# Attention with split-precision products: projection tiles of the next heads two to a pair of steps

## What is computed

```
z = rms_norm(x) @ w_in                      # q, k, v of all heads, gates, ...
q, k = rms_norm(q) * gq, rms_norm(k) * gk   # per head
c = cumsum(log_sigmoid(f + b))              # decay
s = q @ k.T * scale + (c[q] - c[k]), causal
attn = softmax(s) @ v
gates = g_a, g_b = two blocks of 1024 columns of z (sigmoid later)
```

## Time and profile before

| | |
|---|---|
| median of three runs | 1944.1 us (1943.78 to 1945.9) |
| profiled execution | 1945.08 us, span in the trace 1943.4 us |
| TensorE products busy | 1894.3 us, 97% of the span, 11188 instructions |
| VectorE, ScalarE, GpSimd busy | 962.5, 677.1, 520.9 us (50, 35, 27%) |
| TensorE on the chain that ended last | 83% |
| granted clock of TensorE | 0.999 |
| mean traffic | 92 GB/s |

### The profile page before, as it was taken

The page is one execution under the profiler, slowest core; times in us unless marked ns, Lnnn a source line. Parts: engine busy times, 40 slices in busy tenths (PEclk is TensorE's granted clock), DMA queues, the critical chain, the costliest instruction groups (busy, mean ns, idle before and its releaser), DMA issues.

```text
span 1943.4 us, 30986 instructions
## 1 busy us (share of the span) xinstructions
PE 1894.3 (97%) x11188; PEld 1746.3 (90%) x11188; DVE 962.5 (50%) x2296; ACT 677.1 (35%) x1487; POOL 520.9 (27%) x525
## 2 busy tenths in 40 slices
PE   5999999999999999999999999999999999999998
PEld 4999999999888889998889999999998888999986
DVE  5546665653265335545444565665433643455531
ACT  5344444444233223113224444444433332221210
POOL 3623343332031113212134233333311211131110
PEclk9999999999999999999999999999999999999999
DMA  5231313123225323625314113131322342227141
GB/s 157 57 109 49 94 52 98 53 71 88 80 59 141 91 62 87 202 80 172 105 50 116 52 48 100 45 107 49 104 62 62 92 137 77 77 86 232 39 173 54
DMA packets 217803, 178.39 MB, mean 92 GB/s; under 512 B 50260, under 2 KB 191076, under 8 KB 217652
## 3 DMA queue, kind: packets, MB, share of 16 engines
q1 hardware_dynamic: 217652, 176.41, 31.2%
HBM read 131.65 MB, written 44.71 MB: 91 GB/s over the span
## 4 chain that ended last, share of the span: by engine, by line
PE 83%; DVE 5%; issue 4%; DMA 3%; ACT 3%; POOL 1%; SPq 1%; POOLq 0%; DVEq 0%; ACTq 0%
PE bank L76 22%; PE bank L78 21%; PE bank L77 21%; PE bank L1345 3%; PE bank L1359 2%; PE bank L1305 2%; PE bank L1358 2%; PE bank L1328 2%; PE bank L2128 2%; PE bank L1330 2%; PE bank L2151 1%; DVE sg_sT L1583 1%; DMA at_stage<-in_w_in 1%; DVE at_prob L1225 1%; PE bank L2116 1%
## 5 line engine op out<-in xcount | busy, mean ns | idle before, releaser
L76 PE MATMUL bank<-keep_hhi,at_fhi 128*128 128x384 f32 (+1 forms) x768 | 257.1, 335 | 4.3 <-ACT at_th L993 4.0
L78 PE MATMUL bank<-keep_hhi,at_flo 128*128 128x384 f32 (+1 forms) x768 | 251.3, 327 | 0.0
L77 PE MATMUL bank<-keep_hlo,at_fhi 128*128 128x384 f32 (+1 forms) x768 | 251.3, 327 | 0.0
L76 PE MATMUL bank<-aw_whi,keep_hhi 128*128 128x384 f32 (+3 forms) x576 | 198.5, 345 | 3.2 <-ACT at_th L993 1.3
L76 PE MATMUL bank<-keep_hhi,bw_whi 128*128 128x384 f32 (+1 forms) x576 | 195.1, 339 | 2.6 <-DVE br_th L2016 2.6
L77 PE MATMUL bank<-aw_wlo,keep_hhi 128*128 128x384 f32 (+3 forms) x576 | 195.5, 339 | 0.0
L78 PE MATMUL bank<-aw_whi,keep_hlo 128*128 128x384 f32 (+3 forms) x576 | 195.2, 339 | 0.0
L77 PE MATMUL bank<-keep_hlo,bw_whi 128*128 128x384 f32 (+1 forms) x576 | 188.4, 327 | 0.0
L78 PE MATMUL bank<-keep_hhi,bw_wlo 128*128 128x384 f32 (+1 forms) x576 | 188.3, 327 | 0.0
L1039 ACT ACTIVATE at_prob<-at_prob,at_nmx 128x128 f32<-128x128 f32 (+7 forms) x128 | 99.5, 778 | 238.5 <-DVE at_nmx L1232 238.4
L76 PEld LDWEIGHTS bank<-keep_hhi,at_fhi 128*128 128x128 f32 x768 | 144.4, 188 | 7.7 <-ACT at_th L993 6.4
(11 more groups left out here) (252 smaller groups left out, 4283.9 us busy)
## 6 DMA issues: line engine op xcount, KB each, us to landing
at_stage<-in_w_in SPq DMA_DIRECT2D x160, 128.0 KB, 2.3
mg_gate<-gates SPq DMA_DIRECT2D x32, 544.0 KB, 6.2
gates<-at_th SPq DMA_DIRECT2D x64, 192.0 KB, 2.3
br_stage<-in_w_in SPq DMA_DIRECT2D x40, 256.0 KB, 3.2
at_stage<-in_w_in SPq DMA_DIRECT2D x48, 192.0 KB, 2.7
at_decay<-ncum SPq DMA_DIRECT2D x16, 512.0 KB, 3.7
br_k<-in_cache_k SPq DMA_DIRECT2D x32, 256.0 KB, 3.1
br_v<-in_cache_v SPq DMA_DIRECT2D x32, 256.0 KB, 2.9
```

The lines of the kernel that those rows point to most:

```text
L76: nc.tensor.matmul(out, sh, mh, start=start and i == 0, stop=False)
L77: nc.tensor.matmul(out, sh, ml, start=False, stop=False)
L78: last = nc.tensor.matmul(out, sl, mh, start=False, stop=stop and i == n - 1)
```

## The change

For head pairs 1 to 3 the nine projection tiles are due at the steps 3, 5, 7 ... 19 of 24 before, and at 11, 11, 13, 13, 15, 15, 17, 17, 19 after. The X of a tile is due with the next tile, as before, so two X are now due in some pairs. The first of them stays in front of the following T, the second goes behind the two T. W and Y keep their steps (their rule counts from the last tile's step, 19 in both). P moves by itself, by the straight-line rule.

```diff
@@ -679,7 +679,7 @@
     for p in range(1, PAIRS):
-        at = [3, 5, 7, 9, 11, 13, 15, 17, 19]
+        at = [11, 11, 13, 13, 15, 15, 17, 17, 19]
         for t, n in zip(range(NT - len(at), NT), at):
@@ -699,11 +699,13 @@
     for n in range(0, len(steps) + LAG, 2):
         due = after.pop(n, []) + after.pop(n + 1, [])
-        plan += turned
+        plan += turned[:1]
+        second = turned[1:]
         turned = [s for s in due if s[0] == "X"]
         scores = [s for s in due if s[0] == "S"]
         projections = [s for s in due if s[0] == "Z"]
         plan += [("T",) + s for s in steps[n:n + 2]]
+        plan += second
         fill.read(0)
```

## The result

| | before | after |
|---|---|---|
| median of four executions | 1944.0 us (1943.8 to 1945.9) | 2064.2 us (2061.0 to 2070.0) |
| ratio of the runs | 1 | 1.062 (95% interval 1.061 to 1.063) |
| span of the profiled execution | 1943.4 us | 2063.3 us |
| TensorE busy, mean granted clock | 1894.3 us, 0.999 | 1932.8 us, 0.979 |

What follows compares the result with a forecast made beforehand. TensorE, nearly never idle, was taken as the bound, each new wait adding in full. 48.8 + 16.4 + 6.2 + 9.0 = 80.4 us on a 1943.4 us span gave, after small corrections, 2024.5 us; range 1994 to 2042.

Steps and rivals of the forecast that it cites:

- What bounds the kernel: Attention, layers 0 and 1: TensorE nearly never idle, 8.4 us at most to win; each new wait adds in full.
- One sign of being wrong altogether: TensorE's busy time was forecast unchanged; a change in the busy sum would make the prediction wrong altogether.
- Part 1, the second X: X2, X4, X6 wait for the previous X's low part: 8.14 us per 24 steps, six times, 48.8 us.
- taking would have given 40.2: Second-X cost using the 3.13 us chain where GpSimd has nothing queued behind X, instead of 3.61 us: 40.2 us.
- Part 2, thin pairs: Pairs at 20 to 24 lack P, so T waits for late ScalarE and VectorE: 16.4 + 6.2 us; bounds 0, 32.
- the 0.3 us on the half output: In the thin pairs, 0.3 us more for a later wait on the head's half output, beside the 3.8 us wait.
- no P at 22: Claim that the filler, ahead after five dense pairs, puts no P at 22, where two or three stood before.
- Part 3, pairs filled with P: At n = 2, 6, 32 two G splits share a pair, delaying the tanh: 9.0 us both layers; bounds 0, 20.
- the rival that I gave 0.03: TensorE's clock at half rate for the P piece behind each of 14 waits over 3 us: 28 us, 2052; chance 0.03.
- only the second X costs: Rival: ScalarE's backlog is absorbed since TensorE arrives later everywhere; 40 to 49 us, 1984 to 1993; chance 0.12.
- the second X is hidden behind two T: Not-slower rival: low part comes within 1.23 us of the first X; near 1940 us; chance 0.04.
- The third, ScalarE blocked by loads in the filled pairs: Rival: loads block ScalarE's queue in all filled pairs, or late engines drag on; 101 us, about 2045; chance 0.10.

Runs made afterwards that it cites:

- The run with the low part first: Changed kernel, VectorE taking the low parts of an X ahead of evacuating the projection tile directly before it; TensorE's order kept: 2022.8 us (1.041).
- G later: Changed kernel with each split of gate weights listed behind the next pair's T and tanh reads instead of directly behind its P: 2044.3 us (1.051).
- W later: Changed kernel with splits of projection and value weights (W, Y) behind the next pair's T copies instead of ahead of them: 2050.4 us (1.053).
- the filled waits: Changed kernel with 12 or 10 additional 128x512 products on TensorE directly ahead of each second X, results overwritten: 2047.1 us (1.052).
- the artificial ones: Kernel before with ten TensorE waits added per layer, each for 12 or 22 GpSimd writes: 1962.2 us (1.009) and 2002.3 us (1.029).

## Why the prediction was right or wrong

**What bounds the kernel: right.** Each new wait of TensorE was added in full; the account above closes within 0.5 us. One sign of being wrong altogether did come: I had said that the busy time is unchanged, and it grew by 38.5 us. The products are the same; the clock and the hidden parts of the waits made them longer.

**Part 1, the second X: right, to the term.** 8.14 us for 24 steps, 48.8 us; measured 2.82 + 2.28 + 2.27 and three times 0.25, 48.7 us for all six. The rows to read it from were those of the rows phase's end, where the same order of tiles already stood; taking would have given 40.2. In all 18 of these waits `ms` takes 0.63 us and ends with `zg`. That fits the Trainium skill's rule on the port pair that VectorE and GpSimd share (SBUF — State Buffer, "Who interferes with whom"), by which the one that comes second is blocked until the other's instruction is over. No run takes `zg` out of the way, so the 8.6 us that this makes of the 48.8 rest on the durations alone. The run with the low part first shows the main cause: the order on VectorE.

**Part 2, thin pairs: mechanism right, size too high.** 22.6 us forecast, 15.1 measured. In layer 0 the three waits were 3.24, 1.10 and 2.48 us idle, 0.25 us more each with the hidden part, against 3.8, 3.8 and 3.1; the 0.3 us on the half output didn't come. The second is short because the list has one P at n = 46 after all: I carried "no P at 22" from the first 24 steps to the second, where the filler has caught up. The first, at 240.83, is as told:

```profile
238.02 1.35 ACT L970 ACTIVATE aw_whi<-at_stage 128x392 fp32r<-128x392 f32 x3
...
238.99 1.27 DVE L1151 TENSOR_TENSOR aw_wlo<-at_stage,aw_whi 128x392 fp32r<-128x392 f32 x1
...
239.84 0.55 ACT L1051 ACTIVATE at_pthi<-bank 128x256 fp32r<-128x256 f32 x2
...
240.83 0.92 PE L1347 MATMUL bank<-keep_ident,at_prob 128*128 128x128 f32 x4 [3.24 <-DVE at_ptlo L1243]
```

**Part 3, pairs filled with P: mechanism right, far too small.** 9.0 us forecast, 24.2 measured, above my own upper bound of 20. The one wait that I worked out is there, 1 us longer in layer 0 (4.18 us and the hidden 0.25 against 3.4; 2.94 us idle in layer 1). The release came where I had it (141.1 forecast), though I took 136.58, where the second half of the load starts to be issued in the earlier trace rows, for its end. TensorE was there 0.6 us sooner than I had it:

```profile
134.40 0.62 ACT L977 ACTIVATE at_fhi<-at_stage 128x512 fp32r<-128x512 f32 x1
...
139.26 0.63 ACT L977 ACTIVATE at_fhi<-at_stage 128x512 fp32r<-128x512 f32 x1 [3.08 <-DMA at_stage<-in_w_in]
139.79 1.06 ACT L1051 ACTIVATE at_pthi<-bank 128x512 fp32r<-128x512 f32 x2
...
140.75 0.82 ACT L995 ACTIVATE at_th<-bank 128x320 f32<-128x320 f32 x2
...
141.24 0.45 PE L76 MATMUL bank<-keep_hhi,at_fhi 128*128 128x384 f32 x1 [4.18 <-ACT at_th L995]
```

What failed is the choice of places. I asked where two G fall into one pair, and took 0.7 us for n = 6 and 32, which show 0.26 us and nothing in layer 0. The other waits lie at n = 26, 28, 48 and 52: 1.2, 2.3, 1.1 and 2.1 us in layer 0, and 1.3, 1.9, 0.6 and 3.3 us in layer 1. Before those at 28 and 52 ScalarE stands again at a G whose load hasn't landed, as at the first, though the two G are in different pairs:

```profile
259.92 0.63 ACT L977 ACTIVATE at_fhi<-at_stage 128x512 fp32r<-128x512 f32 x1 [2.59 <-DMA at_stage<-in_w_in]
...
379.77 0.63 ACT L977 ACTIVATE at_fhi<-at_stage 128x512 fp32r<-128x512 f32 x1 [4.25 <-DMA at_stage<-in_w_in]
```

At 26 and 48 W copies, at 26 with a G behind them, stand ahead of the T copies and the tanh. The runs with G later and with W later took 16.3 and 11.1 of the 20.9 us that had come, more than there was together, so both kinds of entry hold up the same queue and no single one is the cause.

**The clock: the rival that I gave 0.03 came true.** I priced it at 14 waits and 28 us on top; it is 18 falls and 30.8 us. That these are so close is luck: of my 14 waits eight had a fall and six had none, nine of the falls stand behind waits that I hadn't counted (eight of them behind the X waits of 2.3 us idle), and each took 1.7 us, not 2.0. The step that failed is the sentence that such waits don't occur amid dense work and that the question is open: open should have meant far more than 0.03, and my bound for the forecast should have held it. 1944 + 80 + 28 = 2052 stood in the text, outside my own range. Without the falls the other terms as measured give 1944 + 89.5, near 2034 us, within it: the clock, put at nothing in the sum, is the term that failed. The Trainium skill (TensorE: Matmul & The Clock Gate, "Part 1: The HAM clock gate") says that the clock falls after idleness and rises with activity; the filled waits, with 1.00 behind them, and the artificial ones, with 0.50 behind 4.66 us, agree with it.

**The sum.** 80.4 forecast; - 0.1 (second X) + 15.2 (tanh) - 7.5 (thin pairs) + 1.5 (`at_mx`) + 30.8 (clock) = 120.3.

**Rivals.** That only the second X costs is refuted by the T and tanh waits; that the second X is hidden behind two T, by 3.75 us from X to X. The third, ScalarE blocked by loads in the filled pairs, came true in part: 24.2 us there, but only 15.1 in the thin pairs where it had up to 32.

## What to carry to other kernels

When an engine's own queue is the bound, price each new wait as its length and, for TensorE, what the clock takes behind it: here up to 1.7 us behind every wait over 3 us and behind more than half of those from 2 to 3 us, seldom below 2. Two uses of one single buffer need the whole evacuation chain between them, 3.76 us here, and the chain is read in the list of each engine in it, not in TensorE's. A filler that balances a total leaves some stretches bare: look at what the in-order helpers (here ScalarE) have queued there.

## What the runs showed of the hardware

- TensorE's clock fell to 0.50 for about 3.4 us behind waits, whoever caused them. Of the waits in all traces of this study (behind the rows phase, by their idle time), 29 of 29 over 3 us had a fall, 20 of 31 from 2.6 to 3 us, 40 of 74 from 2.0 to 2.6 us, 5 of 159 from 1 to 2 us. The fall began during the wait or, but for one case at 2.2 us, up to 1.7 us behind it; each one had a wait of 0.5 us or more beside it. The same wait of 2.82 us has a fall behind it at 309.55 and none at 194.44 in one trace, so it isn't the length alone that decides; what does was not tried.
- The executions of the kernel after spread more: 2061 to 2070 us, against 1943.8 to 1945.9 before. That the same waits are followed by a fall in one execution and not in another would explain it, but each kernel has the trace of one execution only, so this isn't shown.
- The record of the granted clock can miss a low stretch. At the program's start eight transposes take 1.97 us in both traces (and at 20.77 after). The clock of 19 to 43 us is 1.00 in the trace of before and 0.50 in that of after:

```profile
19.00:43.00 24.00, 16.91 (x69) 14.32 (x70) 18.75 (x28) 14.94 (x32) 10.80 (x14) 1.00 0.50 132
```

```profile
19.00:43.00 24.00, 16.49 (x66) 14.20 (x66) 17.76 (x26) 13.94 (x29) 9.90 (x13) 0.50 0.50 127
```

The durations are the surer witness of the two. The executions of the kernel before tell the same: their mean granted clock is 0.993 to 0.995 in some and 0.999 to 1.000 in others, with no difference in time (1942 to 1947 us in both groups). 24 us at 0.50 in 1943 would make 0.994.
